# Separate regions for the pool_w loads, and a planner that models one transfer queue for each issuing engine

## What is computed

```python
h = rmsnorm(x, norm1_g)
proj = jnp.einsum("ntd,dc->ntc", h, w_in)              # 1024 -> 2560
u, q, k, v, gb, gc, gh = jnp.split(proj, cuts, axis=-1)
y_pool = pool_mix(pool_hist, u, pos, pool_w, pool_scale)   # windows 2/4/8/16, a 64x64 product each
...                                                    # three dilated sliding-window attentions,
y_attn = jnp.sum(wts[..., None] * jnp.stack(outs, axis=0), axis=0)
y_conv = gb * conv_mix(conv_hist, gc * gh, conv_w)
mixed = jnp.concatenate([y_pool, y_attn, y_conv], axis=-1)
x = x + jnp.einsum("ntc,cd->ntd", mixed, w_out)        # 768 -> 1024
hf = jnp.einsum("ntd,df->ntf", rmsnorm(x, norm2_g), w_up)
x = x + jnp.einsum("ntf,fd->ntd", jnp.square(jax.nn.relu(hf)), w_down)
```

## Time and profile before

| | |
|---|---|
| median of 3 runs | 1660.68 us (1659.42 to 1662.44) |
| the profiled execution | 1659.64 us |
| span of its slowest core (core 1) | 1657.8 us |
| spans of the eight cores | 1642.6 to 1657.8 us |
| mean granted PE clock of the cores | 0.950 to 0.954 |
| PE busy | 1479.5 us, 89% |
| DVE, ACT, POOL busy | 47%, 35%, 18% |
| layer 0: start to the end of the tail | 0 to 410 us |
| layer 0: MLP, and start of layer 1 | from 410 us |
| layer 1: tail ends, MLP begins | 1195.7 us |

### The profile page before, as it was taken

The page is one execution under the profiler, slowest core; times in us unless marked ns, Lnnn a source line. Parts: engine busy times, 40 slices in busy tenths (PEclk is TensorE's granted clock), DMA queues, the critical chain, the costliest instruction groups (busy, mean ns, idle before and its releaser), DMA issues.

```text
span 1657.8 us, 28294 instructions; the slowest of 8 cores (1642.6 to 1657.8 us)
## 1 busy us (share of the span) xinstructions
PE 1479.5 (89%) x9430; PEld 773.7 (47%) x9430; DVE 784.6 (47%) x1210; ACT 582.3 (35%) x1267; POOL 292.5 (18%) x524
## 2 busy tenths in 40 slices
PE   1659998289999999999998999848999999999998
PEld 0346566144444444444454656624444444444443
DVE  1356755257443434444554575625644344344343
ACT  2276555248111212113554555534811121211211
POOL 2417544200000000001015664420000000000000
PEclk9879999589999999999999999958999999999999
DMA  5940015893824205006334002489342510500022
GB/s 147 113 127 2 8 31 108 148 233 57 138 102 81 60 13 107 6 4 90 114 79 83 1 2 38 103 140 247 60 119 102 93 47 13 105 7 4 26 89 93
DMA packets 91943, 130.26 MB, mean 79 GB/s; under 512 B 28920, under 2 KB 62194, under 8 KB 91418
## 3 DMA queue, kind: packets, MB, share of 16 engines
q0 software_dynamic: 59904, 54.07, 23.1%
q1 hardware_dynamic: 30986, 52.50, 9.5%
q10 hardware_dynamic: 912, 21.88, 4.5%
HBM read 159.64 MB, written 44.75 MB: 123 GB/s over the span
## 4 chain that ended last, share of the span: by engine, by line
PE 82%; DMA 6%; ACT 4%; issue 3%; DVE 3%; POOL 1%; ACTq 0%; DVEq 0%; POOLq 0%
PE psum L675 80%; DMA big<-c 4%; DMA big<-pool_w 2%; ACT big L808 1%; PE psum L827 1%; DVE big L816 1%; PE psum L1211 1%; DMA big<-w_in 0%; ACT big L831 0%; ACT big L1264 0%; ACT big L810 0%; DVE big L1553 0%; PE psum L1389 0%; ACT big L1185 0%; POOL big L1177 0%
## 5 line engine op out<-in xcount | busy, mean ns | idle before, releaser
L675 PE MATMUL psum<-big 128*128 128x512 bf16 (+8 forms) x8546 | 1417.7, 328 | 73.4 <-DMA big<-w_in 18.1
L675 PEld LDWEIGHTS psum<-big 128*128 128x128 bf16 (+3 forms) x8546 | 715.4, 103 | 750.3 <-issue 142.4
L1578 ACT ACTIVATE big<-psum 128x512 f32<-128x512 f32 (+1 forms) x320 | 164.7, 518 | 676.4 <-PE psum L675 664.3
L1580 DVE TENSOR_TENSOR big<-psum,big 128x512 bf16<-128x512 f32 (+1 forms) x320 | 187.6, 591 | 279.1 <-ACT big L1578 277.1
L1603 DVE TENSOR_TENSOR big<-psum,big 128x512 f32<-128x512 f32 (+1 forms) x272 | 187.8, 691 | 243.8 <-PE psum L675 243.6
L816 DVE SCALAR_TENSOR_TENSOR big<-big 128x1024 bf16<-128x1024 f32 (+1 forms) x68 | 86.6, 1281 | 58.2 <-ACT big L812 57.5
L735 POOL DMA_DIRECT2D big<-w_up x16 | 12.1, 762 | 489.1 <-PE psum L675 346.2
L827 PE MATMUL psum<-big 128*128 128x128 bf16 (+1 forms) x544 | 45.9, 238 | 45.1 <-DVE big L816 30.7
L808 ACT ACTIVATE big<-big 128x1024 bf16<-128x1024 f32 (+1 forms) x68 | 71.7, 1054 | 30.3 <-DVE big L1603 21.5
L831 ACT COPY big<-psum 128x1024 bf16<-128x1024 bf16 (+1 forms) x68 | 64.2, 971 | 43.9 <-PE psum L827 43.4
L827 PEld LDWEIGHTS psum<-big 128*128 128x128 bf16 (+1 forms) x544 | 37.3, 107 | 58.4 <-issue 52.9
(11 more groups left out here) (80 smaller groups left out, 652.6 us busy)
## 6 DMA issues: line engine op xcount, KB each, us to landing
big<-xp SPq DMA_DIRECT2D x32, 512.0 KB, 9.1
big<-w_up POOLq DMA_DIRECT2D x16, 1024.0 KB, 13.9
big<-w_down POOLq DMA_DIRECT2D x16, 1024.0 KB, 15.6
kv_s<-c ACTq DMA_DIRECT2D x8, 2040.0 KB, 9.1
xpark<-big SPq DMA_DIRECT2D x16, 512.0 KB, 3.1
big<-xpark SPq DMA_DIRECT2D x16, 512.0 KB, 19.7
yp<-big SPq DMA_DIRECT2D x16, 512.0 KB, 2.6
big<-c POOLq DMA_DIRECT2D x26, 256.0 KB, 6.2
```

The costliest lines, as they stand in the source:

```text
L675: S.op("pe", lambda e: e.matmul(out, lhsT=lhsT, rhs=rhs, start=start, stop=stop, skip_group_check=skip), reads=reads, writes=writes, cost=n)
L1578: S.op("act", lambda e: e.activation(out=RL[ri][:, 0:L], in_=bank(pi)[:, 0:L], func=AF.Relu), reads=[("ps", pi)], writes=[("rl", ri)], cos ...
L1580: S.op("dve", lambda e: e.tensor_tensor(out=at[:, fc, 0:L], in0=bank(pi)[:, 0:L], in1=RL[ri][:, 0:L], op=ALU.mult), reads=[("ps", pi), ("r ...
```

## The change

It has four parts.

1. The model of transfers gets a queue for each of the three issuing engines (`sp`, `pool`, `act`), each with 110.0e3 bytes per microsecond, in place of one queue with 190.0e3 for all. The model takes no part in the program that runs; it only changes which task the planner takes next.
2. `PWBD` is registered as four regions, and each of the four pool_w loads writes its own, with its own semaphore. The memset of `PWBD` writes all four, and the matmul at L964 (L967 after) reads all four.
3. The cast to `IDB` stands behind DVE's memsets at the start instead of ahead of them.
4. The call that adds the load of the first piece of `w_in` stands ahead of `load_consts` and `load_smalls`. Its priority is not given, so it is the number of tasks added so far; those of the other two are -49 and -48.

```diff
-DMA_RATE = 190.0e3
+DMA_RATE = {"sp": 110.0e3, "pool": 110.0e3, "act": 110.0e3}
...
-        self.dma_ft = max(self.dma_ft, t + 0.7) + nbytes / DMA_RATE
-        o.end = self.dma_ft + 1.5
+        self.dma_ft[queue] = max(self.dma_ft[queue], t + 0.7) + nbytes / DMA_RATE[queue]
+        o.end = self.dma_ft[queue] + 1.5
...
-    PWBD = ca.take([2, 128], BF16, "pwbd")
+    PWBD = ca.take([2, 128], BF16)
+    K_PW = [("pwbd", i) for i in range(4)]
+    for k_ in K_PW:
+        S.region(k_)
...
     S.dma(lambda e: e.dma_start(out=IDF, in_=c_ident), writes=["idf"], slot="c0")
-    S.op("dve", lambda e: e.tensor_copy(out=IDB, in_=IDF), reads=["idf"], writes=["idb"])
...
-    S.op("dve", lambda e: e.memset(PWBD, 0.0), writes=["pwbd"])
+    S.op("dve", lambda e: e.memset(PWBD, 0.0), writes=K_PW)
...
     S.op("dve", lambda e: e.memset(YS, 0.0), writes=["ys"])
+    S.op("dve", lambda e: e.tensor_copy(out=IDB, in_=IDF), reads=["idf"], writes=["idb"])
...
-                  writes=["pwbd"], slot="pwbd", queue="pool", nbytes=16384)
+                  writes=[("pwbd", g)], slot=("pwbd", g), queue="pool", nbytes=16384)
...
+    load_wa(0, 0)
     R_.add(load_consts(), -49)
     R_.add(load_smalls(0), -48)
-    load_wa(0, 0)
     load_wq(0, 0)
```

More of the change, by code:

```diff
@@ L74, in __init__ @@
         self.ft = {e: 0.0 for e in COMPUTE + ("sp",)}
-        self.dma_ft = 0.0
+        self.dma_ft = {"sp": 0.0, "pool": 0.0, "act": 0.0}
         self.last_end = 0.0
@@ L963, in pool_item @@
         yield "pe"
-        mm(bank(po)[:, 0:L], PWBD[:, pc, :], DTB[pc][:, 0:L], True, True, ["pwbd", kdt], [("ps", po)], pe(L))
+        mm(bank(po)[:, 0:L], PWBD[:, pc, :], DTB[pc][:, 0:L], True, True, K_PW + [kdt], [("ps", po)], pe(L))
         yield "act"
```

## The result

The changed kernel takes 1701.99 us in the median of its runs (1700.25 us is the fastest) against 1661.56 us for the kernel before: the ratio is 1.0244, 95% interval 1.0221 to 1.0267. It is slower by 40 us. The forecast was 1654 us in a range up to 1680 us; the time lies outside it and on the other side.

What follows compares the result with a forecast made beforehand. PE, busy 1479.5 of 1657.8 us, was taken as the bound, so only its idle time at the start and phase A's ends could change: 1659.64 - 30 + 6.5 + 17 = 1653.1, median 1.0 above, 1654 us; range 1634 to 1680.

Steps and rivals of the forecast that it cites:

- Part 1: Start: pool_w waits go, w_in is issued at about 6.5 us, PE's first projection comes at 25, 17 us gained.
- The length of the stream: Start: some 42 us of w_in loads beginning at 6.5 us, delayed by x and constants, would end at 61.
- The later cast of IDB: Start: 0.3 us of DVE long before the first transpose, worth nothing.
- The first rival: Start: w_in is held back like the third pool_w load, PE starts at 36 or 37; 1671 us, chance 0.28.
- The loads of x: Start: they share the DMA engines with w_in, so the first norm tiles' transposes end later, 25 instead of 23.9 us.
- the rule cited above: DMA generally: transfers from different engines share 16 DMA engines; several issuers save only start time, so three modelled queues are wrong.
- Part 2: Start of layer 0: twelve norm tiles stand between projections instead of in a lump, gaining 13 of at most 16.5 us.
- Parts 3 and 4: Ends of phase A: chunks and gain move behind the w_out products, net +6.5 us in layer 0, +17 in layer 1.
- X, gain and the rest of the products: Layer tails: X loads from tile 8 on start after the last chunk, the gain comes last; 25 us in each layer.
- The chunk term: Layer tails: chunks left bare behind the products, four in layer 0 for 14 us, six in layer 1 for 20.6.
- What leaves the attention: Attention before the tails: load waits and chunk chains go, 28 us less in layer 0, 25 less in layer 1.
- Part 4's "0": Layer 1: pool_w waits also go, but POOL had nothing urgent behind them, so 0; the moved call also adds nothing.

Runs made afterwards that it cites:

- e1: The changed kernel with the planner's transfer model as before (one queue, 190.0e3), the rest of the change kept: ratio 0.9879 to the kernel before.
- e13: The kernel before with the four pool_w regions alone; old model, cast and call as before: ratio 1.0044 to the kernel before.
- e6: The changed kernel with the q and k gain loads reading 128 different identity rows instead of one row 128 times (gains wrong): ratio 1.0172 to the kernel before.
- e2: The kernel before with the new three-queue model of transfers alone; pool_w stays one region: ratio 1.0094 to the kernel before.
- e11: The changed kernel with its three modelled queues at 250.0e3 each instead of 110.0e3: ratio 1.0158 to the kernel before.
- e10: The changed kernel with one modelled queue at 250.0e3 in place of three at 110.0e3: ratio 0.9816 to the kernel before.

## Why the prediction was wrong, point by point

**Part 1, the start: failed, and it is the largest miss (26.5 of 47 us).** Alone it turns the forecast from -6.5 to +20; the miss of the tails alone would have turned it too, to +10.7. The step that failed was "not w_in: ... it would be there at 15, ... at 23", and from it "25 for the first projection". The first piece did land at 21.7 (17.3 after its issue at 4.4), within what was written. But the changed kernel's stream begins with the q/k/v projections, which wait for pieces two to four. Two and three landed at 24.6 and 26.4, the fourth at 41.2. I priced w_in by its first piece and did not ask which piece PE's first matmul reads, though PE's order after begins with `128x256` rows and before with `128x512` ones. e1 shows both halves: 24.76 for the matmuls of the first piece, 41.78 for the others.

The length of the stream was wrong as well. I had its end at 61 us; it came at 84.9, and in the median of the cores at 83.0 (73.8 in the kernel before).

**The later cast of IDB was not nothing.** It let the four pool_w loads be issued at 2.18 us instead of the 4.3 that I took, and w_in at 4.38 instead of 6.5; e13, without it, has 4.20 and 6.40. In the window from 23.9 to 41.9 us I also called POOL idle, and it was busy 8.92 us, with the issue of w_in.

**The first rival had the right mechanism and the wrong weight.** It said that something between 20 and 30 us holds back another queue, and named the q and k gains among the suspects; e6 shows that it is the reading of one row 128 times. What I wrote against it, that w_in is issued before those loads, is true of all thirteen pieces (the last is issued at 14.8 us, the first gain at 20.4) and did not help: what had not landed by then waited beside them. Its price was too small as well, since it took only the start to be lost and left the tails at their sizes: 1671 us.

**The loads of x**, which I had allowed for as "slower by the same sharing" and priced at 1 us, became later, but not where I looked. The fourth tile's load landed 1.3 us later in the median of the cores (15.5 and 14.2). Its transposes begin at 26.45 instead of 21.78, and that is the new order and no transfer. In e2, where w_in is issued as late as before, they begin just as late, and in e1, with w_in early, at 22.50:

```profile
26.85 1.01 PE L827 MATMUL psum<-big 128*128 128x128 bf16 x8 [4.37 <-DVE big L816]
```

In the changed kernel and in e2 ACT's stream has a copy of a finished tile ahead of the second square, where it had the second square first. It is SP's later loads that the early w_in delays: xs lands at 43.4 us in the median, 30.4 in the kernel before and 29.3 in e2, and ACT waits for it, in the changed kernel and then in e2:

```profile
ACT big L811 <- DMA big<-xs: 16.4, 1, 16.4
```

```profile
ACT big L808 <- DMA big<-xs: 3.0, 1, 3.0
```

PE had projections to do from 41.4 to 51.6, so this wait is not seen there. The issue itself slowed down: the nine conv_w loads took SP 10.20 us to issue where they took 4.41 (4.87 in e2, 8.78 in e1). The early transfers of POOL's queue were paid for by SP's. This agrees with the rule cited above (the Trainium skill, DMA: Bandwidth & Descriptors, "Issuing engines are not separate DMA queues"), by which transfers of all engines run on the same 16 DMA engines and interleave. That three modelled queues at the right rate cost 3.5% against one (e11 and e10) fits it, but is one draw of the orders.

**Part 2, the norms between the projections: half right.** The lump is gone and PE's work up to the first chunk rose from 54.4 to 62.3 us in about the same time, so some 11 us were won of the 30 that parts 1 and 2 allowed together, with the -3.5 included; as the first projection came only 0.5 us earlier, nearly all of it belongs to the 13 of part 2. The statement in the section on the change that as much projection work lies behind the mark in both was off by these 8 us.

**Parts 3 and 4, the tails: right in mechanism, sign and order, too small in size.** Term by term in layer 0: products 31.5 predicted, 30.7 measured; chunks 14, measured 23.4; X, gain and the rest of the products 25, measured 20.7; norms 37, measured 42.6. The chunk term is the mis-sized one: one chunk takes 2.6 to 3.1 us, about as said, but 4.7 us of waiting for loads, 3.1 us for the sample's result and 3.7 us for the first tile of X came on top, which I had put under the next term or nowhere. In layer 1 the same: 27.7, 33.0, 21.3 and 40.3 against 31.5, 20.6, 25 and 37. What leaves the attention was right within some 6 us in both layers (-33.5, with the 8 us of the start in it, where -28 stood, and -18.8 where -25 stood).

**What was not in the sum: the clock behind the tails.** PE's mean clock is 0.63 in the norms of layer 0 and the first 186 matmuls of the dense MLP take 233 ns each (43.25 us), where a 512-wide one takes 217 ns in the earlier trace rows (24.34 us for 112). In that stretch the clock rises:

```profile
417.12:422.00 4.88, 4.88 (x15) 1.78 (x13) 3.45 (x6) 2.91 (x6) 0.00 (x0) 0.50 0.88 110
422.00:430.00 8.00, 8.00 (x36) 3.44 (x35) 2.62 (x5) 2.39 (x4) 0.00 (x0) 0.93 0.06 6
```

From 430 us on it is 1.00. In the kernel before it was 1.00 already in the last 15 us of the tail. That makes the MLP stretch of layer 0 some 3 us longer (186 matmuls at 233 ns instead of 217); layer 1 begins its MLP at 0.59 and its last stretch is 2.7 us longer.

**Part 4's "0" for pool_w in layer 1 and for the moved call** hold: no engine waits for a pool_w load any more, and POOL's stream begins as before.

## What to carry to other kernels

When a load is moved forward, look up which piece of it the first waiting instruction reads, and price that piece, not the first one that lands. When a planner sets the streams, a change of its costs, or of anything that shifts its clock by a microsecond or two, is a new draw of the orders: here the same edit gained 21 us in one kernel and lost 11 in another at the dense MLP of layer 0, so a part is priced only by a run whose streams are otherwise equal. And in a tail, the load on which a whole chain depends (here the gain of the norms) must not be left to a tie in the planner: one priority was worth some 50 us, 17.5 of them in a tail that compares cleanly.

## What the runs showed of the hardware

Loads that read one row of 256 bytes 128 times leave the DMA engines half idle, and other queues wait with them: 58 GB/s at a share of 0.53 for 16 us, against 185 GB/s at 1.10 when the same number of pieces of the same size come from different rows. In the kernel before the four loads landed 3 to 4 us apart (21.1, 24.8, 28.4 and 31.5 us), and the third pool_w load, issued among them, took its 14.29 us; in e6 they are 1 to 2 us apart. The broadcast of a row of 4096 bytes (the gain of the norms, 512 KB in all) landed 6.3 us after its issue at the start of the changed kernel. I had not expected that the source's address could matter so much for so few bytes (128 KB).

SP's issue of transfers is slower while w_in is in flight: nine loads of 0.5 KB took it 4.41 us to issue in the kernel before and 4.87 in e2, 8.78 in e1 and 10.20 in the changed kernel. What holds the issue back no run shows.
